# A decoder step on one core: the output projection as three products of split operands, its weights loaded and split in eight pieces

## The chip, the core and the metric

The kernel runs on one core of a Trainium2 chip, as one program with one launch. The metric is the device time of that program in microseconds, the median over the runs shown. PE is the matrix engine (TensorE), PEld its loads of the stationary operand, DVE the vector engine, ACT the scalar engine, POOL GpSimd, and SP the queue engine that issues most transfers.

## What is computed

One decoder layer over 1,024 prompt tokens and 8 sample tokens, in float32, width 1,024. Cut to the part around the change:

```python
h = rmsnorm(x, norm1_g)
sq, sk, sv, dq, dk, dv, ga, gb = project_inputs(h, pos, w_in, qn_g, kn_g)
o_sb  = sb_attn(sq, sk, sv, sb_bias)          # stick-breaking attention
o_dil = dil_attn(dq, dk, dv)                  # dilated windows
y_a = o_sb  @ w_br_a
y_b = o_dil @ w_br_b
x = x + (ga * y_a + gb * y_b) @ w_out         # <- the output projection, [1032 x 1024] @ [1024 x 1024]
x = x + moe(rmsnorm(x, norm2_g), ...)         # router, top 8 of 64 experts, shared expert
```

The change touches only how the product with `w_out` is computed, and how `w_out` comes into SBUF.

## The kernel before, in words

The program is a row of stages, each a block of its own with a barrier of all engines at its end: `phase_project` (input projection), `phase_windows` and `phase_stick` (attention), `phase_gate` (gates and the two branch products), `phase_out` (output projection, second norm, router logits), `phase_route` (top-k and the table of blocks), `phase_experts`, `phase_finish`. A stage can't begin, its transfers included, before the one ahead of it has ended.

**Float32 products in two ways.** Where a matmul takes float32 operands, the trace has two records for each matmul instruction. Where the operands are of the type `F32R` (fp32r in the rows), it has one. Three stages use `F32R` already, in the same pattern: ACT writes a rounded copy `hi` of an operand, DVE writes `lo = raw - hi`, and PE adds three products, hi x hi, hi x lo and lo x hi, into one PSUM tile. These are the input projection (lines 562 to 564, weights in `wring`, 128 x 512 outputs), the gates (lines 1460 to 1462) and the down product of the experts (line 2199).

**`phase_out` (from line 1550).** There are NT = 9 tiles of tokens, eight of 128 rows and a last one of 8. `mixT` holds the gated mix, already turned, as KC = 8 chunks of 128 contraction rows. It lies in the large buffer `turned`, as `h2T` does. The work of a tile `t`:

- PE, line 1630: for both halves `k` of the 1,024 output columns and all 8 chunks `c`, one float32 matmul with the stationary operand `mixT[:, c, tile]` and the moving operand `wo[:, c, 512 columns]`, into `pY[t % 2]`: 16 matmuls, thus 32 records. Then it signals `y_ready`.
- DVE, line 1687: `x1 = pY + x`, with the rows of `x` loaded again from DRAM (line 1603). ACT, line 1658: sum of squares of `x1`; line 1660: square root. DVE, line 1689: reciprocal; line 1693: `h2`.
- SP, lines 1608 and 1609: `x1` and `h2` to DRAM.
- PE, line 1640: eight transposes of `h2` into `pT`; ACT, line 1665: copy to `h2T`. PE, line 1647: router logits of the tile, 8 float32 matmuls of 64 columns.

PE's program runs as: products of tile `t`, transposes of tile `t - 1`, logits of tile `t - 2`. Before the products of `t >= 2` it waits for `x1` of tile `t - 2`, which frees the half of `pY`.

**How the stage begins.** SP issues one transfer for the whole of `w_out` (4 MB, line 1591), one for the gain of the norm (0.5 MB once broadcast, line 1592), one for the router weights (0.25 MB, line 1593), then two stores of zero rows (0.64 MB each, lines 1595 and 1596), then the `x` rows of tiles 0 and 1. The first three share one semaphore, and PE waits for all of it (`pe.wait_ge(w_in, 48)`) before its first matmul. ACT and DVE have nothing to do until tile 0 is through PE. POOL writes three small constants.

Of the kernel before, what the change touches and what calls it, by code (L numbers as in the profile page):

```python
# [49 lines left out]
def rows_of(t):  # L50
    return P if t < NT - 1 else NS
# [19 lines left out]
def build(nc, a, o):  # L71
# [22 lines left out]
    with ExitStack() as ctx:  # L94
        sb = lambda name, shape, dt=F32: ctx.enter_context(nc.sbuf_tensor(name, shape, dt))
        held = []

        def semaphore(name):
            held.append(nc.alloc_semaphore(name=name))
            return held[-1]  # L100

        scratch["semaphore"] = semaphore
        ident = sb("ident", [P, P])
        scores = sb("scores", [P, NT, E])
        expert_row = sb("expert_row", [1, NBLK + 1], I32)
        slot_info = sb("slot_info", [P, NBLK, 4], I32)
        with ExitStack() as attention:
            turned = attention.enter_context(nc.sbuf_tensor("turned", [P, 20, S], F32))
            phase_project(nc, a, o, scratch, ident, turned)
            odT = attention.enter_context(nc.sbuf_tensor("odT", [P, GW // P, T], F32))  # L110
            phase_windows(nc, a, o, scratch, ident, turned, odT)
            oT = attention.enter_context(nc.sbuf_tensor("oT", [P, SBH // 2, T], F32))
            phase_stick(nc, a, o, scratch, ident, turned, oT)

            nc.clear_and_free_semaphores(held)
            nc.all_engine_barrier()
            phase_gate(nc, a, o, scratch, turned, oT, odT)
            phase_out(nc, a, o, scratch, ident, turned, scores)
            phase_route(nc, a, o, scratch, ident, turned, scores, expert_row, slot_info)
        phase_experts(nc, a, o, scratch, ident, expert_row, slot_info)  # L120
        phase_finish(nc, a, o, scratch)
# [1428 lines left out]
def phase_out(nc, a, o, sc, ident, turned, scores):  # L1550

    flat = turned[:, :, :].rearrange("p a b -> p (a b)")
    h2T = flat[:, :KC * T].rearrange("p (c t) -> p c t", c=KC)
    mixT = flat[:, KC * T:2 * KC * T].rearrange("p (c t) -> p c t", c=KC)
    with ExitStack() as ctx:
        sb = lambda name, shape, dt=F32: ctx.enter_context(nc.sbuf_tensor(name, shape, dt))
        sem = sc["semaphore"]
        wo = sb("w_o", [P, KC, D])
# [5 lines left out]
        junk = sb("junk2", [P, D])  # L1564
        zero = sb("zero_row", [BLK // 5, D])
# [7 lines left out]
        w_in = sem("o_w_in")  # L1573
# [14 lines left out]
        with nc.Block() as block:  # L1588
            @block.sync
            def _(sp):  # L1590
                sp.dma_start(wo[:, :, :], a["w_out"][0].rearrange("(c p) n -> p c n", p=P)).then_inc(w_in, 16)
                sp.dma_start(gain[:, :], a["norm2_g"].broadcast_to([P, D])).then_inc(w_in, 16)
                sp.dma_start(wr[:, :, :], a["w_router"][0].rearrange("(p c) n -> p c n", c=KC)).then_inc(w_in, 16)
                sp.wait_ge(set_up, 3)
                sp.dma_start(sc["h2"][T:, :].rearrange("(p n) d -> p n d", n=5), zero[:, :].unsqueeze(1).broadcast_to([BLK // 5, 5, D])).then_inc(zero_out, 16)
                sp.dma_start(sc["x2"][T:, :].rearrange("(p n) d -> p n d", n=5), zero[:, :].unsqueeze(1).broadcast_to([BLK // 5, 5, D])).then_inc(zero_out, 16)
# [17 lines left out]
            @block.gpsimd  # L1614
            def _(pool):
                pool.memset(eps[:, :], EPS).then_inc(set_up, 1)
                pool.memset(zero[:, :], 0.0).then_inc(set_up, 1)
                pool.memset(scores[:, :, :], 0.5).then_inc(set_up, 1)

            @block.tensor  # L1620
            def _(pe):
                pe.wait_ge(w_in, 48)
                for t in range(NT + 2):
                    if t < NT:
                        m = rows_of(t)
                        if t >= 2:
                            pe.wait_ge(x1_ready, t - 1)
                        for k in range(2):
                            for c in range(KC):
                                last = pe.matmul(pY[:m, t % 2, k * 512:(k + 1) * 512], mixT[:, c, t * P:t * P + m], wo[:, c, k * 512:(k + 1) * 512],  # L1630
                                                 start=(c == 0), stop=(c == KC - 1))
                        last.then_inc(y_ready, 1)
# [10 lines left out]
                    if u >= 0:  # L1643
                        m = rows_of(u)
                        pe.wait_ge(h2T_ready, u + 1)
                        for c in range(KC):
                            last = pe.matmul(pR[:m, u // 8, (u % 8) * E:(u % 8 + 1) * E], h2T[:, c, u * P:u * P + m], wr[:, c, :],
                                             start=(c == 0), stop=(c == KC - 1))
# [3 lines left out]
            def _(act):  # L1652
                act.wait_ge(set_up, 3)
                for t in range(NT + 1):
                    if t < NT:
                        m = rows_of(t)
                        act.wait_ge(x1_ready, t + 1)
                        act.activation(junk[:m, :], x1[:m, t % 2, :], ACT.Square, accum_out=ss[:m, t:t + 1]).then_inc(ss_ready, 1)
                        act.wait_ge(ss_ready, t + 1)
                        act.activation(rms[:m, t:t + 1], ss[:m, t:t + 1], ACT.Sqrt, scale=1.0 / D, bias=eps[:m, :]).then_inc(rms_ready, 1)  # L1660
                    if t >= 1:
# [9 lines left out]
            def _(dve):  # L1671
# [8 lines left out]
                dve.wait_ge(w_in, 48)  # L1680
                for t in range(NT):
# [8 lines left out]
                    if t >= 2:  # L1690
# [3 lines left out]
                                             by_chunk(gain[:m, :]), ALU.mult, ALU.mult).then_inc(h2_ready, 1)  # L1694

# [683 lines left out]
```

## Time and profile before

| | before |
|---|---|
| median of 3 runs | 2507.28 us (2506.61 to 2510.26) |
| the profiled execution, its own time | 2507.1 us |
| span of its trace | 2505.3 us |
| PE busy | 2216.6 us, 88% of the span |
| DVE, ACT, POOL busy | 1013.7, 684.4, 802.8 us |
| granted TensorE clock, mean | 0.933 |
| `phase_out` in the trace | from 1210.9 to 1381.4 us |
| products of line 1630 | 256 records of 128 x 512 and 32 of the last tile |

Times in the rows are in microseconds from the start of the span unless marked ns. "Busy" is the time in which an engine had at least one instruction under way; matmuls overlap, so the spacing of their starts is their pace, and the duration of one is longer than that. The granted clock is given as a share of 2.4 GHz: 1.00 is 2.4 GHz and 0.50 is 1.2 GHz.

### The profile page before, as it was taken

To read this page: it belongs to the slowest core of one execution; us is meant where nothing else is said; L and a number is where in the kernel's file an instruction comes from. 1 tells how busy PE (TensorE), PEld (TensorE's weight loads), DVE (VectorE), ACT (ScalarE), POOL (GpSimd) and SP (SyncE) were. 2 spreads that over 40 slices of the span, in tenths; PEclk is the share of its full clock that TensorE was granted. 3 is DMA by queue.
4 is the path that set the end of the run, shared out by engine and by line. 5 is a ranking of instruction groups with operands and counts; after the bars stand their busy time and mean duration, and the time that the engine had idled before them with its cause. 6 is when DMAs were issued, how large, how long until landed. Compare 5 with 4: busy or idle time off the path is not lost. (4 is left out here: it accounts for less than half of the span.)

```text
span 2505.3 us, 35857 instructions
## 1 busy us (share of the span) xinstructions
PE 2216.6 (88%) x13110; PEld 1737.1 (69%) x13110; DVE 1013.7 (40%) x1695; ACT 684.4 (27%) x1156; POOL 802.8 (32%) x784
## 2 busy tenths in 40 slices
PE   7998499888599979999799771999999999999994
PEld 6776477677344438898454531898989888898983
DVE  4576778766354442111022441333333333333331
ACT  6221122145254542111011000233333333323231
POOL 2000033102555530111000074454545454555542
PEclk9999799958799989999899895999999999999997
DMA  6576611063345528881331143899999999999996
GB/s 209 190 233 213 219 34 35 29 200 121 126 135 160 159 83 288 281 281 42 135 108 61 57 136 133 273 326 318 327 324 321 324 321 322 320 328 316 326 314 175
DMA packets 182418, 520.08 MB, mean 208 GB/s; under 512 B 22942, under 2 KB 81752, under 8 KB 155880
## 3 DMA queue, kind: packets, MB, share of 16 engines
q1 hardware_dynamic: 137040, 369.24, 43.2%
q0 software_dynamic: 34912, 89.87, 14.3%
q10 hardware_dynamic: 10368, 59.73, 7.1%
q8 instruction: 55, 0.90, 0.2%
q14 instruction: 43, 0.35, 0.1%
HBM read 442.32 MB, written 124.65 MB: 226 GB/s over the span
## 5 line engine op out<-in xcount | busy, mean ns | idle before, releaser
L2182 PE MATMUL pG_e<-xT,w_e 128*128 128x160 f32 x4224 | 627.5, 302 | 2.4 <-issue 1.3
L2182 PEld LDWEIGHTS pG_e<-xT,w_e 128*128 128x128 f32 x4224 | 586.8, 197 | 29.4 <-issue 25.9
L2282 DVE TENSOR_TENSOR w_e_lo<-w_e,w_e_hi 128x2048 fp32r<-128x2048 f32 x66 | 151.4, 2294 | 342.0 <-ACT w_e_hi L2229 342.0
L562 PE MATMUL pP<-wring,hT_hi 128*128 128x512 f32 (+2 forms) x576 | 229.2, 398 | 45.9 <-DVE wring L498 43.5
L563 PE MATMUL pP<-wring,hT_hi 128*128 128x512 f32 (+2 forms) x576 | 223.9, 389 | 0.0
L564 PE MATMUL pP<-wring,hT_lo 128*128 128x512 f32 (+2 forms) x576 | 223.8, 389 | 0.0
L2131 POOL DMA_INDIRECT x_scratch<-y_e,target x66 | 106.7, 1617 | 341.6 <-ACT y_tail L2249 341.6
L2229 ACT ACTIVATE w_e_hi<-w_e 128x2048 fp32r<-128x2048 f32 x66 | 126.1, 1911 | 329.1 <-DMA w_e<-in_w_e_down 329.1
L2272 DVE COPY xT<-pX 128x512 f32<-128x512 f32 x132 | 90.7, 687 | 226.7 <-PE pX L2166 226.7
L355 POOL TENSOR_TENSOR sqr<-stage 128x512 f32<-128x512 f32 (+1 forms) x27 | 29.0, 1074 | 411.9 <-ACT stage L427 411.9
L562 PEld LDWEIGHTS pP<-wring,hT_hi 128*128 128x128 f32 (+1 forms) x576 | 105.9, 184 | 74.8 <-issue 45.0
L1460 PE MATMUL pG<-hg_hi,wg_hi 128*128 128x344 f32 x384 | 130.2, 339 | 16.1 <-DVE hg_lo L1521 16.1
L1630 PE MATMUL pY<-w_o,turned 128*128 128x512 f32 (+1 forms) x288 | 127.2, 601 | 17.9 <-DMA w_r<-in_w_router 17.9
L427 ACT ACTIVATE stage<-pP 128x512 f32<-128x512 f32 (+3 forms) x72 | 41.1, 570 | 338.3 <-PE pP L564 323.0
L2116 POOL DMA_INDIRECT rows<-h_scratch,index x66 | 109.6, 1660 | 54.4 <-POOL index L2113 51.0
L564 PEld LDWEIGHTS pP<-wring,hT_lo 128*128 128x128 f32 (+1 forms) x576 | 105.4, 183 | 29.2
L563 PEld LDWEIGHTS pP<-wring,hT_hi 128*128 128x128 f32 (+1 forms) x576 | 106.1, 184 | 26.7
L1461 PE MATMUL pG<-hg_lo,wg_hi 128*128 128x344 f32 x384 | 124.0, 323 | 0.0
L1462 PE MATMUL pG<-hg_hi,wg_lo 128*128 128x344 f32 x384 | 124.0, 323 | 0.0
L2248 ACT ACTIVATE y_e<-pY_e,target 128x1024 f32<-128x1024 f32 x66 | 73.6, 1115 | 179.8 <-DMA x_scratch<-y_tail,target 175.0
L1630 PEld LDWEIGHTS pY<-w_o,turned 128*128 128x128 f32 (+1 forms) x288 | 51.7, 182 | 87.6 <-issue 69.2
L1547 POOL TENSOR_TENSOR turned<-halves 128x344 f32<-128x344 f32 x24 | 27.8, 1160 | 263.1 <-DVE halves L1540 263.1
(271 smaller groups left out, 3788.9 us busy)
## 6 DMA issues: line engine op xcount, KB each, us to landing
w_e<-in_w_e_gate SPq DMA_DIRECT2D x66, 1024.0 KB, 8.3
w_e<-in_w_e_up SPq DMA_DIRECT2D x66, 1024.0 KB, 13.0
w_e<-in_w_e_down SPq DMA_DIRECT2D x66, 1024.0 KB, 6.8
turned<-in_cache_sb_kv SPq DMA_DIRECT2D x128, 256.0 KB, 3.4
vbuf<-in_cache_sb_kv SPq DMA_DIRECT2D x128, 256.0 KB, 3.0
out<-in_cache_win_kv ACTq DMA_DIRECT2D x8, 4094.0 KB
turned<-in_w_in ACTq DMA_DIRECT2D x56, 256.0 KB, 5.5
turned<-in_w_in SPq DMA_DIRECT2D x16, 512.0 KB, 8.8
```

The costliest lines, as they stand in the source:

```text
L562: pe.matmul(pP[:m, i % 4, :w], hi, w_hi(u), start=(c == 0), stop=False)
L563: pe.matmul(pP[:m, i % 4, :w], hi, w_lo(u), start=False, stop=False)
L564: last = pe.matmul(pP[:m, i % 4, :w], lo, w_hi(u), start=False, stop=(c == KC - 1))
L1460: pe.matmul(pG[:, i % 2, k, :NC], w_hi[:, r, c, :], hT_hi[:, c, cols], start=(c == 0), stop=False)
L1461: pe.matmul(pG[:, i % 2, k, :NC], w_hi[:, r, c, :], hT_lo[:, c, cols], start=False, stop=False)
L1462: last = pe.matmul(pG[:, i % 2, k, :NC], w_lo[:, r, c, :], hT_hi[:, c, cols], start=False, stop=(c == KC - 1))
L1630: last = pe.matmul(pY[:m, t % 2, k * 512:(k + 1) * 512], mixT[:, c, t * P:t * P + m], wo[:, c, k * 512:(k + 1) * 512], start=(c == 0), sto ...
L2116: pool.indirect_dma_start(rows[:, r, :], None, sc["h2"], bass.IndirectOffsetOnAxis(ap=index[:, r, 0:1], axis=0)).then_inc(rows_in[r], 16)
L2131: pool.indirect_dma_start(sc["x2"], bass.IndirectOffsetOnAxis(ap=target[:, r, 0:1], axis=0), y[:, :], None, compute_op=ALU.add).then_inc(y ...
L2182: last = pe.matmul(pG[:, k, f * BLK:(f + 1) * BLK], wv[:, c, f, :], xT[:, r, c, :], start=(c == 0), stop=(c == KC - 1))
L2229: act.activation(whi[:, r, :], w[:, r, 2, :], ACT.Copy).then_inc(whi_ready, 1)
L2282: dve.tensor_tensor(wlo[:, r, :], w[:, r, 2, :], whi[:, r, :].bitcast(F32), ALU.subtract).then_inc(wlo_ready, 1)
```

## The change

The product with `w_out` becomes three products of `F32R` operands. ACT writes `wo_hi` and DVE `wo_lo` from the raw weights, chunk by chunk, and for each tile ACT writes `mix_hi` and DVE `mix_lo` from `mixT`, one or two tiles ahead. PE issues 48 matmuls a tile in place of 16. `w_out` is loaded by eight transfers with a semaphore each; in tile 0 PE waits for each chunk's `lo`. PE no longer waits for the gain and the router weights ahead of its first product: DVE waits for the gain ahead of its first `x1`, PE for the router weights ahead of the first logits. The raw weights lie in `turned` now, over the place that `h2T` takes later. To make room, the two attention outputs `odT` and `oT` are freed ahead of `phase_out`, the sum of squares writes its unused result into `h2`, and the zero rows are a part of `h2`; so ACT waits for the stores of the zero rows before it writes `h2` of tile 1.

```diff
@@ build
+            branches.close()
             phase_out(nc, a, o, scratch, ident, turned, scores)
@@ phase_out
+    wo = flat[:, :KC * D].rearrange("p (c n) -> p c n", c=KC)
-        wo = sb("w_o", [P, KC, D])
+        wo_hi = sb("w_o_hi", [P, KC, D], F32R)
+        wo_lo = sb("w_o_lo", [P, KC, D], F32R)
+        mix_hi = sb("mix_hi", [P, 2, KC, P], F32R)
+        mix_lo = sb("mix_lo", [P, 2, KC, P], F32R)
-        junk = sb("junk2", [P, D])
-        zero = sb("zero_row", [BLK // 5, D])
+        zero = h2[:BLK // 5, 1, :]
@@ sync
-                sp.dma_start(wo[:, :, :], a["w_out"][0].rearrange("(c p) n -> p c n", p=P)).then_inc(w_in, 16)
-                sp.dma_start(gain[:, :], a["norm2_g"].broadcast_to([P, D])).then_inc(w_in, 16)
-                sp.dma_start(wr[:, :, :], a["w_router"][0].rearrange("(p c) n -> p c n", c=KC)).then_inc(w_in, 16)
+                for c in range(KC):
+                    sp.dma_start(wo[:, c, :], a["w_out"][0, c * P:(c + 1) * P, :]).then_inc(w_in[c], 16)
+                sp.dma_start(gain[:, :], a["norm2_g"].broadcast_to([P, D])).then_inc(gain_in, 16)
+                sp.dma_start(wr[:, :, :], a["w_router"][0].rearrange("(p c) n -> p c n", c=KC)).then_inc(wr_in, 16)
@@ tensor
-                pe.wait_ge(w_in, 48)
                 for t in range(NT + 2):
                     if t < NT:
                         m = rows_of(t)
+                        pe.wait_ge(mlo_ready, t + 1)
                         if t >= 2:
                             pe.wait_ge(x1_ready, t - 1)
-                        for k in range(2):
-                            for c in range(KC):
-                                last = pe.matmul(pY[:m, t % 2, k * 512:(k + 1) * 512], mixT[:, c, t * P:t * P + m], wo[:, c, k * 512:(k + 1) * 512],
-                                                 start=(c == 0), stop=(c == KC - 1))
+                        for c in range(KC):
+                            if t == 0:
+                                pe.wait_ge(wlo_ready, c + 1)
+                            terms = ((mix_hi, wo_hi), (mix_hi, wo_lo), (mix_lo, wo_hi))
+                            for n, (mt, wt) in enumerate(terms):
+                                for k in range(2):
+                                    last = pe.matmul(pY[:m, t % 2, k * 512:(k + 1) * 512], mt[:, t % 2, c, :m], wt[:, c, k * 512:(k + 1) * 512],
+                                                     start=(c == 0 and n == 0), stop=(c == KC - 1 and n == 2))
                         last.then_inc(y_ready, 1)
...
                         pe.wait_ge(h2T_ready, u + 1)
+                        if u == 0:
+                            pe.wait_ge(wr_in, 16)
@@ scalar
+                def high_mix(t):
+                    m = rows_of(t)
+                    if t >= 2:
+                        act.wait_ge(y_ready, t - 1)
+                    act.activation(mix_hi[:, t % 2, :, :m], mixT[:, :, t * P:t * P + m], ACT.Copy).then_inc(mhi_ready, 1)
+
+                high_mix(0)
+                for c in range(KC):
+                    act.wait_ge(w_in[c], 16)
+                    act.activation(wo_hi[:, c, :], wo[:, c, :], ACT.Copy).then_inc(whi_ready, 1)
+                high_mix(1)
...
-                        act.activation(junk[:m, :], x1[:m, t % 2, :], ACT.Square, accum_out=ss[:m, t:t + 1]).then_inc(ss_ready, 1)
+                        if t == 1:
+                            act.wait_ge(zero_out, 32)
+                        act.activation(h2[:m, t % 2, :], x1[:m, t % 2, :], ACT.Square, accum_out=ss[:m, t:t + 1]).then_inc(ss_ready, 1)
...
+                    if t + 2 < NT:
+                        high_mix(t + 2)
@@ vector
-                dve.wait_ge(w_in, 48)
+                def low_mix(t):
+                    m = rows_of(t)
+                    dve.wait_ge(mhi_ready, t + 1)
+                    if t >= 2:
+                        dve.wait_ge(y_ready, t - 1)
+                    dve.tensor_tensor(mix_lo[:, t % 2, :, :m], mixT[:, :, t * P:t * P + m], mix_hi[:, t % 2, :, :m].bitcast(F32),
+                                      ALU.subtract).then_inc(mlo_ready, 1)
+
+                low_mix(0)
+                for c in range(KC):
+                    dve.wait_ge(whi_ready, c + 1)
+                    dve.tensor_tensor(wo_lo[:, c, :], wo[:, c, :], wo_hi[:, c, :].bitcast(F32), ALU.subtract).then_inc(wlo_ready, 1)
+                low_mix(1)
+                dve.wait_ge(gain_in, 16)
...
+                    if t + 2 < NT:
+                        low_mix(t + 2)
```

## Rows read from the trace of the kernel before

**Rows 1.** The page: span and number of instructions.
```profile
span 2505.3 us, 35857 instructions
```

**Rows 2.** Groups by line and shape, 1208 to 1382 us: busy us, mean ns, idle ahead.
```profile
L1630 PE MATMUL pY<-w_o,turned 128*128 128x512 f32 x256 | 113.3, 602 | 17.9 <-DMA w_r<-in_w_router 17.9
L1647 PE MATMUL pR<-w_r,turned 128*128 128x64 f32 x128 | 17.0, 291 | 0.0
L1693 DVE SCALAR_TENSOR_TENSOR h<-x,rstd,gain 128x1024 f32<-128x1024 f32 x8 | 16.1, 2006 | 0.3
L1630 PE MATMUL pY<-w_o,turned 128*8 128x512 f32 x32 | 13.9, 592 | 0.0
```

**Rows 3.** Timeline of the stage: start, duration, instruction, idle time ahead of it.
```profile
1210.88 0.37 SPq L1591 DMA_DIRECT2D w_o<-in_w_out  x1
1226.47 29.61 PE L1630 MATMUL pY<-w_o,turned 128*128 128x512 f32 x64 [17.86 <-DMA w_r<-in_w_router]
1242.45 1.22 DVE L1687 TENSOR_TENSOR x<-pY,x_again 128x1024 f32<-128x1024 f32 x1 [32.86 <-PE pY L1630]
1248.77 0.33 SPq L1608 DMA_DIRECT2D x_scratch<-x  x1
1270.73 1.23 DVE L1687 TENSOR_TENSOR x<-pY,x_again 128x1024 f32<-128x1024 f32 x1 [9.63 <-PE pY L1630]
1287.13 1.23 DVE L1687 TENSOR_TENSOR x<-pY,x_again 128x1024 f32<-128x1024 f32 x1 [11.43 <-PE pY L1630]
```

**Rows 4.** Timeline of line 1630's loads: clock 0.50 first, then 1.00.
```profile
1229.20 0.34 PEld L1630 LDWEIGHTS pY<-w_o,turned 128*128 128x128 f32 x1 [0.52 <-issue]
1230.05 0.31 PEld L1630 LDWEIGHTS pY<-w_o,turned 128*128 128x128 f32 x1 [0.52 <-issue]
...
1238.33 0.19 PEld L1630 LDWEIGHTS pY<-w_o,turned 128*128 128x128 f32 x1 [0.24 <-issue]
...
1255.07 0.19 PEld L1630 LDWEIGHTS pY<-w_o,turned 128*128 128x128 f32 x1 [0.24 <-issue]
```

**Rows 5.** Timeline of PE in the input projection, clock 1.00, first and twentieth product.
```profile
99.78 0.40 PE L563 MATMUL pP<-wring,hT_hi 128*128 128x512 f32 x1
...
104.18 0.39 PE L564 MATMUL pP<-wring,hT_lo 128*128 128x512 f32 x1
```

**Rows 6.** Timeline of loads where the input projection begins, from second to twelfth product.
```profile
17.52 0.33 PEld L563 LDWEIGHTS pP<-wring,hT_hi 128*128 128x128 f32 x1
...
21.79 0.28 PEld L564 LDWEIGHTS pP<-wring,hT_lo 128*128 128x128 f32 x1
```

**Rows 7.** Groups by line of ACT and DVE, 935 to 1208 us: the gates' splits.
```profile
L1478 ACT ACTIVATE wg_hi<-turned 128x1024 fp32r<-128x1024 f32 x15 | 15.8, 1057 | 75.6 <-PE pG L1462 71.9 <-issue 3.3 <-DMA turned<-in_w_in 0.4
...
L1516 DVE TENSOR_TENSOR wg_lo<-turned,wg_hi 128x1024 fp32r<-128x1024 f32 x15 | 18.3, 1222 | 54.3 <-ACT wg_hi L1478 54.3
```

**Rows 8.** Stretches from 1210 us: length, the five engines' busy us, PEclk, DMA share, GB/s.
```profile
1210.00:1214.10 4.10, 0.00 (x0) 0.00 (x0) 0.00 (x0) 0.00 (x0) 2.07 (x4) 0.89 0.46 140
1210.00:1223.00 13.00, 0.00 (x0) 0.00 (x0) 0.00 (x0) 0.00 (x0) 2.07 (x4) 0.62 0.84 326
1210.00:1225.20 15.20, 0.00 (x0) 0.00 (x0) 0.00 (x0) 0.00 (x0) 2.07 (x4) 0.61 0.86 327
1210.00:1230.60 20.60, 4.13 (x5) 1.82 (x6) 0.00 (x0) 0.00 (x0) 2.07 (x4) 0.59 0.90 333
```

**Rows 9.** Transfers issued from 1208 to 1260 us: KB each, median us to landing.
```profile
h_scratch<-zero_row SPq DMA_DIRECT2D x1, 640.0 KB, 15.7
```

**Rows 10.** Issue to landing of ten stores into `x_scratch`: nine of x1, one of zeros.
```profile
DMA to landing us min/median/max: 2.6/2.7/16.6
```

**Rows 11.** Stretches of other stages, columns as in Rows 8.
```profile
1600.00:2020.00 420.00, 420.00 (x3105) 377.71 (x3104) 142.88 (x181) 128.40 (x153) 211.25 (x182) 1.00 1.00 322
```

**Rows 12.** Stretch of the input projection, products of line 562 alone.
```profile
250.00:300.00 50.00, 21.00 (x72) 13.40 (x72) 0.78 0.77 243
```

**Rows 13.** Who PE waited for, 1500 us to the end: total, times, longest.
```profile
PE pX L2166 <- DMA rows_tail<-h_scratch,index: 11.5, 1, 11.5
```

More of the change, by code:

```diff
@@ L109, in build @@
             phase_project(nc, a, o, scratch, ident, turned)
-            odT = attention.enter_context(nc.sbuf_tensor("odT", [P, GW // P, T], F32))
+            branches = ctx.enter_context(ExitStack())
+            odT = branches.enter_context(nc.sbuf_tensor("odT", [P, GW // P, T], F32))
             phase_windows(nc, a, o, scratch, ident, turned, odT)
-            oT = attention.enter_context(nc.sbuf_tensor("oT", [P, SBH // 2, T], F32))
+            oT = branches.enter_context(nc.sbuf_tensor("oT", [P, SBH // 2, T], F32))
             phase_stick(nc, a, o, scratch, ident, turned, oT)
@@ L1572, in phase_out @@
         pR = ctx.enter_context(nc.psum_tensor("pR", [P, 2, 512], F32))
-        w_in = sem("o_w_in")
+        w_in = [sem(f"o_w_in{c}") for c in range(KC)]
+        gain_in = sem("o_gain_in")
+        wr_in = sem("o_wr_in")
+        whi_ready = sem("o_whi_ready")
+        wlo_ready = sem("o_wlo_ready")
+        mhi_ready = sem("o_mhi_ready")
+        mlo_ready = sem("o_mlo_ready")
         x_in = [sem(f"o_x_in{i}") for i in range(2)]
@@ L1590, in _ @@
             def _(sp):
-                sp.dma_start(wo[:, :, :], a["w_out"][0].rearrange("(c p) n -> p c n", p=P)).then_inc(w_in, 16)
-                sp.dma_start(gain[:, :], a["norm2_g"].broadcast_to([P, D])).then_inc(w_in, 16)
-                sp.dma_start(wr[:, :, :], a["w_router"][0].rearrange("(p c) n -> p c n", c=KC)).then_inc(w_in, 16)
+                for c in range(KC):
+                    sp.dma_start(wo[:, c, :], a["w_out"][0, c * P:(c + 1) * P, :]).then_inc(w_in[c], 16)
+                sp.dma_start(gain[:, :], a["norm2_g"].broadcast_to([P, D])).then_inc(gain_in, 16)
+                sp.dma_start(wr[:, :, :], a["w_router"][0].rearrange("(p c) n -> p c n", c=KC)).then_inc(wr_in, 16)
                 sp.wait_ge(set_up, 3)
-                sp.dma_start(sc["h2"][T:, :].rearrange("(p n) d -> p n d", n=5), zero[:, :].unsqueeze(1).broadcast_to([BLK // 5, 5, D])).then_inc(zero_out, 16)
-                sp.dma_start(sc["x2"][T:, :].rearrange("(p n) d -> p n d", n=5), zero[:, :].unsqueeze(1).broadcast_to([BLK // 5, 5, D])).then_inc(zero_out, 16)
+                sp.dma_start(sc["h2"][T:, :].rearrange("(p n) d -> p n d", n=5), zero.unsqueeze(1).broadcast_to([BLK // 5, 5, D])).then_inc(zero_out, 16)
+                sp.dma_start(sc["x2"][T:, :].rearrange("(p n) d -> p n d", n=5), zero.unsqueeze(1).broadcast_to([BLK // 5, 5, D])).then_inc(zero_out, 16)
                 for t in range(NT + 1):
@@ L1616, in _ @@
                 pool.memset(eps[:, :], EPS).then_inc(set_up, 1)
-                pool.memset(zero[:, :], 0.0).then_inc(set_up, 1)
+                pool.memset(zero, 0.0).then_inc(set_up, 1)
                 pool.memset(scores[:, :, :], 0.5).then_inc(set_up, 1)
```

## The prediction

> **What bounds the kernel now.** I read the profile in this order: the page for the span [rows 1], the groups by line within `phase_out` for the size of the product [rows 2], then the timeline of the stage for what ends each wait [rows 3, 4].
>
> The stage has two parts. In the first, PE stands idle: the load of `w_out` is issued at 1210.88, and PE's first product starts at 1226.47, after an idle stretch that the transfer of `w_r` ended [rows 3]. `w_r` is the last of three transfers behind one semaphore. In the second, PE is the bound without a gap: the 32 records of a tile follow each other, and DVE's sum of tile 0 starts at 1242.45, of tile 2 at 1270.73, of tile 3 at 1287.13 [rows 3]. So the period is 16.40 us. DVE sat idle 11.43 us of it until PE was done [rows 3]. Whatever shortens PE's tile shortens the stage, until another chain fills the period.
>
> **Pace before.** At clock 1.00 the loads of line 1630 that start at 1238.33 and at 1255.07 have 39 gaps between them, 0.429 us each [rows 4]. Two records make one float32 matmul of 512 columns, 0.858 us, and a tile has 16: 13.73 us. At clock 0.50 the loads are 0.85 us apart (1229.20, 1230.05) [rows 4].
>
> **Pace after.** The same product already runs in the input projection: `F32R`, 128 x 512, hi and lo interleaved. From the first product at 99.78 to the twentieth at 104.18 are 19 gaps, 4.40 us, thus 0.2316 us for each product at clock 1.00 [rows 5]. At clock 0.50, ten gaps from 17.52 to 21.79 give 0.427 us [rows 6]. A tile after the change has 48 such products: 48 x 0.2316 = 11.12 us. The saving is 13.73 - 11.12 = 2.61 us a tile. It holds for the last tile of 8 rows too, as its 32 records took 13.9 us [rows 2]: the 512 moving columns set the time, not the rows.
>
> The Trainium skill ("TensorE: Matmul & The Clock Gate", section "Back-to-back issue gap") gives 512 / 2.4 + 2.5 = 216 ns for one pass at the full clock. By it a tile would take 10.4 us, and the kernel would end some 6 us earlier than I forecast. The row has 231.6 ns for this very pattern, so the row decides.
>
> **Tile 0, term by term.** First the bytes. 0.574 MB had moved by 1214.1 (4.10 us at 140 GB/s), 4.24 MB by 1223.0, 4.97 MB by 1225.2 [rows 8]. The weights are 4.19 MB, and with gain and `w_r` it is 4.98 MB. PE started 1.27 us after 1225.2, which I take for the time from the last byte to the signal. Served in order, piece 0 (0.524 MB) is in at 1214.0 and signalled at 1215.3; piece 7 is in at 1222.9 and signalled at 1224.2; the pieces come 1.27 us apart. That transfers are served in order shows in the store of zero rows, issued behind the weights: 15.7 us to landing for 640 KB [rows 9], where the typical store of 512 KB into the `x1` scratch took 2.7 [rows 10]. SP issues each of the eight in about 0.4 us (0.37 for the one there is) [rows 3], 3 us for all, well ahead of the data.
>
> Each piece then passes ACT and DVE. The gates' splits have the same 128 x 1024 shape: 1.06 us and 1.22 us [rows 7]. Both are below 1.27, so neither engine holds up the row of pieces. The splits of `mixT` for tile 0 (1.06 + 1.22) lie in the time before piece 0 lands. PE starts at 1215.3 + 1.06 + 1.22 + 0.1 = 1217.7. The granted clock fell while PE was idle (mean 0.62 from 1210 to 1223) [rows 8], and PE's first products before the change ran at 0.50 [rows 4]; the same holds here. The slow stretch lasted from 1226.47 to a little after 1230.05 there [rows 3, 4], and 4.7 us where the input projection began [rows 6]; I take 4.2. At 0.427 us that is 9.8 products; the other 38.2 take 8.85 us. PE ends tile 0 at 1217.7 + 4.2 + 8.85 = 1230.8. The data do not hold it up: piece 7 is split at 1224.2 + 2.3 = 1226.5, and its six products need 1.4 us more, thus 1227.9. Before, DVE's sum came at 1242.45, so PE's end was at about 1242.2. Gain on tile 0: 11.4 us.
>
> **What the change adds beside that.**
> - Per tile, ACT's copy of the mix (1.06) and DVE's difference (1.22) [rows 7]. The chain from the sum of tile 0 to the store of its `h2` took 1248.77 - 1242.45 = 6.3 us, with one table load in it [rows 3]. With DVE's 1.22 behind it, `mix_lo` of tile t + 2 is ready 7.6 us after PE has finished tile t. PE asks for it only after tile t + 1, at least 11.1 us later. Cost nothing. The cover is 3.5 us or more: what exceeds it would be paid once a tile.
> - ACT copies `h2T` 1.06 us later, for logits a whole tile away. Nothing.
> - `x` of tile 0 is now wanted 11.4 us earlier. It is behind the same bytes as before: 6.8 MB, and 6.86 had moved by 1230.6 [rows 8], so it is signalled at 1231.9. DVE's first sum is about 1 us late. `h2` of tile 0 is then ready at 1238.2, and PE asks for it at 1230.8 + 11.1 = 1241.9. Hidden, with 3.7 us to spare.
> - ACT waits for the zero rows before it writes `h2` of tile 1. The second of the two is issued at once behind the first (landing at 1228.1 by [rows 9] and the issue at 1212.40), and tile 1 comes at 1242. Nothing. The waits for gain and `w_r` end by 1226.5, ahead of their use.
> - The end of the stage is as it was: no split is left for it. The freeing of `odT` and `oT` moves addresses only.
>
> **What follows the stage.** From 1381 us on, everything is set in motion by the stage's end, and its transfers start with its own block. The loop of the experts is bound by PE (420.00 of 420.00 us busy) with the DMA share at 1.00 [rows 11]; neither sees the change. The gain is carried to the end whole.
>
> **Sum.** 11.4 + 8 x 2.61 = 32.3 us. The profiled execution took 2507.1 us (span 2505.3 [rows 1] and 1.8 around it), 0.2 below the median of the three runs. 2507.1 - 32.3 + 0.2 = 2475.0 us.
>
> **Bounds of the unknowns.** The slow stretch from none to 4.7 us: -1.9 to +0.2 us. The pace of the products: the down product of the experts has the least alike order, some 0.234 us; that is +1 us. Start of PE: 1 us either way. Run to run, those before differ by 3.6 us. So the likeliest case has 2471 to 2479 as its own range.
>
> **Rivals.**
> 1. *Each piece pays for itself.* If eight pieces don't overlap as one transfer does, each costs the 2.7 us of a lone store of this size [rows 10]: the last lands at 1210.9 + 21.6 = 1232.5, and tile 0 ends at 1232.5 + 2.3 + 1.4 = 1236.2, 5.4 us later. Time 2480.4. Against it speaks that DMA ran at share 0.86 up to 1225.2, the quiet start included, over three transfers in a row [rows 8]. Chance 0.09. The Trainium skill ("DMA: Bandwidth & Descriptors", section "Measured (HBM→SBUF, 128 partitions, SWDGE, issued from GpSimd)") says to batch transfers to at least 1 MiB for 75% of peak, which speaks against pieces of 512 KB. It is this rival; [rows 8] don't bear it out for transfers that are queued one behind another.
> 2. *The pieces don't come in order*, so that splitting the load does nothing: the first usable one is signalled with the last, by 1226.4 as `w_r` was [rows 3]. PE starts at 1228.8 and ends tile 0 at 1241.8; the gain there is 0.4 us in place of 11.4. Time 2486. Against it: the late zero rows [rows 9]. Chance 0.07.
> 3. *Slower: the clock is lost.* PE waits piece by piece in tile 0, and later on the splits. The input projection, with the same pattern and waits on splits, had a stretch of 50 us at a granted clock of 0.78 [rows 12]. A product at clock 0.50 costs 0.427 - 0.232 = 0.195 us more. With the clock at 0.50 throughout, the 422 products other than those already counted slow cost 82 us: 2557 us. It turns the sign once 32.3 / 0.195 = 166 of them, three and a half tiles, run slow. Against it: at half clock the six products of a piece take 2.6 us and pieces come each 1.27 us, so PE doesn't wait in tile 0 once started, and later the cover is 3.5 us a tile. Chance 0.03.
> 4. *Given back later.* The experts begin with a wait of 11.5 us for gathered rows [rows 13], and their loop has no DMA to spare [rows 11]. One more such wait: 2486.5. Nothing in the change feeds it. Chance 0.04.
> 5. *Faster than forecast*: a slow stretch near nothing and an earlier first piece, 2470. Chance 0.05.
>
> **Chances and range.** The forecast keeps 0.72. 2470 to 2486 holds it, rival 1 and about half of rivals 2, 4 and 5, some 0.88; its lower end is the fast case and its upper end rival 2, and neither can be drawn in without losing a case. A measurement of this kernel can tell about 0.2%, 5 us, from no change. Faster by more: all cases but rival 3, and of it the part with under 3 tiles slow, less what none of them names: 0.96. Within: 0.01. Slower: 0.03.
>
> **What would show it.** In the profile after: eight loads of `w_out` and PE's first product at about 1217.7, 6.8 us after the first load's issue; the loads of line 1630's successor 0.427 us apart for some ten products and 0.232 from then on; DVE's first sum near 1232; a period of 13.8 us in place of 16.4; no idle PE ahead of `mix_lo`. Wrong would be: a first product after 1224 (rival 2), gaps between the pieces' products at full clock in tile 0 that leave its end after 1233 (rival 1), PEclk under 1.00 in the tiles from 1 on (rival 3), or a stage 32 us shorter with a total that isn't (rival 4).

## The result, and the profile after

| | before | after |
|---|---|---|
| median | 2507.84 us (4 runs, 2506.61 to 2510.26) | 2471.79 us (4 runs, 2470.16 to 2475.73) |
| profiled execution, span | 2507.1, 2505.3 us | 2471.59, 2469.7 us |
| first load of `w_out` to the first transfer of the next stage | 1210.88 to 1381.51: 170.63 us | 1209.36 to 1344.17: 134.81 us |

The ratio is 0.9853, 95% interval 0.9839 to 0.9868: 36 us less. The forecast was 2475.0 in 2470 to 2486.

Of the spans' difference of 35.6 us, 35.8 lie in the stage itself. What is ahead of it was 1.5 us shorter, what follows was 1.7 us longer, and neither is touched by the change. In the kernels below, the stage's own length repeats within about 2 us, while its first load starts anywhere from 1207.7 to 1215.4. So I read the stage, from its first load (times with a plus sign), and the total only with its interval. Each length of a stage below is that of one trace.

The page after, to be read with [rows 1]: there are 346 more instructions, and the granted clock is as it was.

```profile
span 2469.7 us, 36203 instructions
PE 2189.0 (89%) x13254; PEld 1760.6 (71%) x13254; DVE 1033.4 (42%) x1712; ACT 700.6 (28%) x1173; POOL 804.2 (33%) x784
```

Groups by line and shape, 1208 to 1350 us, to be read with [rows 2] and [rows 7]. 256 records of one line have become three times 128; the splits cost what the gates' did; and PE's idle time ahead of the products is 8.5 us in place of 17.9.

```profile
L1646 PE MATMUL pY<-w_o_hi,mix_hi 128*128 128x512 f32 x128 | 40.8, 400 | 8.5 <-DVE w_o_lo L1724 8.5
L1646 PE MATMUL pY<-w_o_lo,mix_hi 128*128 128x512 f32 x128 | 40.0, 394 | 0.0
L1646 PE MATMUL pY<-w_o_hi,mix_lo 128*128 128x512 f32 x128 | 39.9, 393 | 0.0
...
L1724 DVE TENSOR_TENSOR w_o_lo<-turned,w_o_hi 128x1024 fp32r<-128x1024 f32 x8 | 9.8, 1225 | 3.4 <-ACT w_o_hi L1680 3.1
L1733 DVE TENSOR_TENSOR x<-pY,x_again 128x1024 f32<-128x1024 f32 x8 | 9.8, 1225 | 49.7 <-PE pY L1646 44.0 <-DMA x_again<-in_x_prompt 5.5
...
L1680 ACT ACTIVATE w_o_hi<-turned 128x1024 fp32r<-128x1024 f32 x8 | 8.5, 1060 | 4.7 <-DMA turned<-in_w_out 4.7
```

Timeline of the stage after, to be read with [rows 3]:

```profile
1209.36 3.81 SPq L1603 DMA_DIRECT2D turned<-in_w_out  x8
1213.12 1.06 ACT L1680 ACTIVATE w_o_hi<-turned 128x1024 fp32r<-128x1024 f32 x1 [2.67 <-DMA turned<-in_w_out]
1215.58 1.19 PE L1646 MATMUL pY<-w_o_hi,mix_hi 128*128 128x512 f32 x2 [8.47 <-DVE w_o_lo L1724]
...
1222.54 1.06 ACT L1680 ACTIVATE w_o_hi<-turned 128x1024 fp32r<-128x1024 f32 x1 [0.22 <-DMA turned<-in_w_out]
...
1231.54 1.23 DVE L1733 TENSOR_TENSOR x<-pY,x_again 128x1024 f32<-128x1024 f32 x1 [5.54 <-DMA x_again<-in_x_prompt]
1237.98 0.33 SPq L1620 DMA_DIRECT2D x_scratch<-x  x1
1238.92 1.03 PE L1656 MATMUL pT<-ident,h 128*128 128x128 f32 x8
...
1305.27 1.23 DVE L1733 TENSOR_TENSOR x<-pY,x_again 128x1024 f32<-128x1024 f32 x1 [7.46 <-PE pY L1646]
1318.86 1.23 DVE L1733 TENSOR_TENSOR x<-pY,x_again 128x1024 f32<-128x1024 f32 x1 [8.49 <-PE pY L1646]
1332.36 1.21 DVE L1733 TENSOR_TENSOR x<-pY,x_again 8x1024 f32<-8x1024 f32 x1 [8.46 <-PE pY L1646]
...
1344.17 0.36 SPq L1847 DMA_DIRECT2D before_r<-in_before  x1
```

The first piece is at ACT at +3.8 and the eighth at +13.2. ACT takes them in the order of issue, and its wait for each of the eight was ended by a transfer, 1.24 to 1.81 us after the one before, so they also came in that order. PE starts at +6.2; before it was +15.6. The period of a tile is 13.59 us in place of 16.40, and DVE still idles 7.5 us of it until PE is done (8.5 in the last two rows: no split of a later tile is left there). PE is the bound as before. And DVE's first sum waited 5.5 us for the `x` rows. `h2` of tile 0 was on its way out at 1237.98, and PE asked for it at 1238.92: 0.9 us of cover.

Timeline of PE's loads at the stage's start. Each row is two loads; 0.76 for two is clock 0.50, 0.42 is clock 1.00. The slow stretch is seven products long.

```profile
1217.85 0.76 PEld L1646 LDWEIGHTS pY<-w_o_hi,mix_hi 128*128 128x128 f32 x2
1218.70 0.42 PEld L1646 LDWEIGHTS pY<-w_o_lo,mix_hi 128*128 128x128 f32 x2
```

### The profile page after: what moved, and what is told of

Same layout as the page of the kernel before. It is cut to its first block and busy times, and to the rows that moved or that the text cites. A ratio compares the mean times of both kernels' runs of the same rounds, so it can differ in the third digit from the quotient of the medians.

```text
span 2469.7 us, 36203 instructions
## 1 busy us (share of the span) xinstructions
PE 2189.0 (89%) x13254; PEld 1760.6 (71%) x13254; DVE 1033.4 (42%) x1712; ACT 700.6 (28%) x1173; POOL 804.2 (33%) x784
## 5 line engine op out<-in xcount | busy, mean ns | idle before, releaser
L2181 POOL DMA_INDIRECT x_scratch<-y_tail,target x66 | 104.6, 1585 | 20.1 <-issue 20.1
L750 DVE TENSOR_SCALAR low<-pZ,bias 128x512 f32<-128x512 f32 (+3 forms) x96 | 54.9, 613 | 123.2 <-PE pZ L906 123.1
```

## The experiments

The edits stand against the changed kernel, except in the second. Their totals are told beside a run of the kernel before on the same chip.

### One half at a time

One transfer, the three products:

```diff
-                for c in range(KC):
-                    sp.dma_start(wo[:, c, :], a["w_out"][0, c * P:(c + 1) * P, :]).then_inc(w_in[c], 16)
+                sp.dma_start(wo[:, :, :], a["w_out"][0].rearrange("(c p) n -> p c n", p=P)).then_inc(w_in[0], 16)
...
-                    act.wait_ge(w_in[c], 16)
+                    act.wait_ge(w_in[0], 16)
```

> The changed kernel with its weights loaded by one transfer and one semaphore; the three products stay. The changed kernel took 2471.8 us. My theory (two separate gains: an early start worth about 10 us in tile 0, and a shorter PE tile worth 2.8 us in each): PE starts 15.7 us after the stage's first load in place of 6.2, tile 0 ends near 28.3 us after it in place of 18.7, the tiles after it keep their period of 13.6 us, and the time is about 2481. Rival (transfer order: the pieces are no earlier than the whole, PE's early start comes from dropping gain and router weights from the wait): time within 2 us of 2471.8. Rival (the pieces cost transfer time): a little faster than 2471.8.

Eight pieces, the product in float32 (against the kernel before; the loads and the later waits for the gain and the router weights are those of the change):

```diff
-                pe.wait_ge(w_in, 48)
...
-                        for k in range(2):
-                            for c in range(KC):
+                        for c in range(KC):
+                            if t == 0:
+                                pe.wait_ge(w_in[c], 16)
+                            for k in range(2):
```

> The kernel before with only the second half of the change: eight pieces with a semaphore each, chunks outermost on PE, gain and router weights waited for later; the product stays in float32, and there are no splits. My theory: PE starts about 3.8 us after the first load, tile 0 ends at about 19.6 in place of 31.4 us, the tiles after it keep 16.4 us, and the time is 2507.8 - 11.8 = 2496. Together with the run of one load it shows whether the two halves add up: 11.8 + (2507.8 - 2481) = 38.6 would be over the 36 of the whole, since the longer tile 0 hides a little of the load. Rival (the early start is worth something only with the shorter products): 2505 or more.

| | PE's first product | DVE's first sum | stage | total |
|---|---|---|---|---|
| before | +15.6 | +31.6 | 170.6 | |
| three products alone | +15.5 | +28.7 | 144.1 | 2477.9, ratio 0.9869 (0.9852 to 0.9885) |
| eight pieces alone | +3.7 | +21.2 | 159.3 | 2496.0, ratio 0.9942 (0.9925 to 0.9958) |
| the change | +6.2 | +22.2 | 134.8 | 0.9853 (0.9839 to 0.9868) |

Against the kernel before, the products alone shorten the stage by 26.6 us and the pieces alone by 11.3, where the whole has 35.8. The expectation put such a difference down to the length of tile 0. The rows show another reason: both kernels also drop the wait for the gain and the router weights, so it is counted twice. With one transfer, all of `w_out` was there at +13.0 (first row below), where PE had waited until +15.6 before. The dropped wait is thus worth 2.6 us, and in the kernels with three products the two splits of the first chunk take 2.5 back (+13.0 to +15.5). What the pieces give by themselves is 15.5 - 6.2 = 9.3 us, and 144.1 - 134.8 is the same 9.3.

In the first kernel ACT gets its first piece only with the last byte; the idle stretch of PE is back:

```profile
1223.66 5.79 ACT L1679 ACTIVATE w_o_hi<-turned 128x1024 fp32r<-128x1024 f32 x6 [11.93 <-DMA turned<-in_w_out]
...
1226.12 1.19 PE L1645 MATMUL pY<-w_o_hi,mix_hi 128*128 128x512 f32 x2 [17.73 <-DVE w_o_lo L1723]
```

The rival that the early start comes from the dropped wait for gain and router weights falls: this kernel doesn't wait for them either, and starts at +15.5. The total was 2477.9 us where I had expected 2481, and the total alone would not have shown the loss, which is 9.3 us against the first run of the change and 7.4 against its second. The changed kernel run again on another chip had 0.9872 (0.9853 to 0.989), within the interval of this one. The stage showed it.

### PE as the bound: 16, 48 and 64 products

```diff
-                            terms = ((mix_hi, wo_hi), (mix_hi, wo_lo), (mix_lo, wo_hi))
+                            terms = ((mix_hi, wo_hi), (mix_hi, wo_lo), (mix_lo, wo_hi), (mix_lo, wo_lo))
```

> The changed kernel with the fourth product too (lo x lo), 64 in place of 48 a tile. If PE is the bound in each tile: 16 x 0.2265 = 3.6 us more a tile, the period 17.2 us in place of 13.6, in nine tiles 32.6 us, and the time about 2504, near the time of the kernel before. Rival (another chain, the splits or the x rows, sets part of the period of 13.6 us): less than that by the part.

```diff
+                            terms = ((mix_hi, wo_hi),)
```

> The changed kernel with only the product hi x hi, 16 a tile: two of the three terms are left out, so the product with w_out is less exact; all splits are still made. PE's tile is 3.6 us of products and 3.0 of transposes and logits, thus 6.6 us. The rest of the stage then shows what comes next after PE. My theory: the split of tile t + 2 waits for the sum and norm of tile t (about 6.4 us behind it on DVE), and the x rows of tile t + 1 are issued about 7 us after tile t - 1 and take 5.8 us to land, so the period is 6.6 to 7.5 us, and the time is 2471.8 - 8 x 6.5 - (2 to 4) = about 2417. Rival (a chain just under 13.6 us has been hidden by PE): a period over 9 us.

| products a tile | period | stage | total, one run |
|---|---|---|---|
| 16 | 6.34 us | 85.2 | 2425.2 |
| 48 | 13.59 us | 134.8 | |
| 64 | 17.22 us | 168.0 | 2502.5 |

The period falls on one line: (17.22 - 13.59) / 16 = 0.227 us for each product, and (13.59 - 6.34) / 32 = 0.227. So nothing but PE sets the period, over all this range; with 64 products the stage was 33.2 us longer, where 32.6 was expected. Even at 6.34 us PE is without a gap in the steady tiles, where DVE's sum now follows its last one within 0.2 us:

```profile
1259.65 1.03 PE L1656 MATMUL pT<-ident,h 128*128 128x128 f32 x8
1259.85 1.23 DVE L1733 TENSOR_TENSOR x<-pY,x_again 128x1024 f32<-128x1024 f32 x1 [0.21 <-PE pY L1646]
1260.53 1.90 PE L1665 MATMUL pR<-w_r,turned 128*128 128x64 f32 x16
...
1262.23 3.92 PE L1646 MATMUL pY<-w_o_hi,mix_hi 128*128 128x512 f32 x16
```

I had expected 2417 for 16 products, a stage 55 us shorter than in the change; it was 49.6 shorter, and the rest of the eight us between lies outside the stage. What the stage lacks is at its beginning. There, tile 0 and tile 1 gained only 1.1 us together (the second sum at +28.6 in place of +29.8): the loads set tile 0's end, and then PE waited 6.2 us for `h2` of tile 0.

### The x rows late

```diff
+                for i in range(2):
+                    sp.dma_start(pad[:, i, :], a["x_prompt"][0, i * P:i * P + P]).then_inc(pad_in, 16)
```

> The changed kernel with 1 MB more loaded (into a buffer that nothing reads) ahead of the x rows of tile 0. In the change DVE waited for these rows until 1231.54, and the store of h2 of tile 0 was issued at 1237.98, 0.9 us before PE had ended tile 1 and asked for it: the cover was 0.9 us, where I had predicted 3.7. My theory: the rows come 2.7 us later, PE then waits about 1.8 us ahead of the transposes of tile 0, and the stage is longer by that. Rival (the cover is not used up, as PE has other work): no wait ahead of the transposes.

DVE's first sum came at +25.6 in place of +22.2, 3.4 us later. PE waited 2.1 us ahead of the transposes of tile 0. So far as expected. But the stage took 139.6 us, 4.8 more than in the change, not 2. The timeline of PE behind the wait shows the rest:

```profile
1239.64 1.10 PE L1661 MATMUL pT<-ident,h 128*128 128x128 f32 x8 [2.09 <-DVE h L1744]
1240.69 0.93 PE L1651 MATMUL pY<-w_o_hi,mix_hi 128*128 128x512 f32 x2
1241.43 1.05 PE L1651 MATMUL pY<-w_o_lo,mix_hi 128*128 128x512 f32 x2
1242.28 1.05 PE L1651 MATMUL pY<-w_o_hi,mix_lo 128*128 128x512 f32 x2
1243.13 1.05 PE L1651 MATMUL pY<-w_o_hi,mix_hi 128*128 128x512 f32 x2
1243.99 0.85 PE L1651 MATMUL pY<-w_o_lo,mix_hi 128*128 128x512 f32 x2
1244.67 0.63 PE L1651 MATMUL pY<-w_o_hi,mix_lo 128*128 128x512 f32 x2
```

The same in stretches (length, PE, PEld, DVE, ACT, POOL, PEclk, DMA share, GB/s):

```profile
1238.00:1240.00 2.00, 0.35 (x3) 0.36 (x4) 2.00 (x2) 0.33 (x1) 0.00 (x0) 1.00 0.00 0
1240.00:1242.00 2.00, 2.00 (x11) 1.57 (x10) 1.77 (x2) 0.20 (x1) 0.00 (x0) 0.76 0.80 322
1242.00:1244.00 2.00, 2.00 (x7) 1.52 (x6) 0.65 (x2) 1.97 (x4) 0.00 (x0) 0.50 0.98 279
1244.00:1246.00 2.00, 2.00 (x9) 1.64 (x8) 2.00 (x2) 1.14 (x2) 0.00 (x0) 0.88 0.46 186
```

Behind a wait of 2.1 us and small transposes the granted clock went from 1.00 to 0.50 and came back some 3 us later, and that cost about as much again as the wait: the transposes of tile 0 were 2.3 us later than in the change (+31.9 against +29.6), and DVE's sum of tile 2 was 4.25 us later (+45.8 against +41.5), so 1.9 us came from the slow products. The last half microsecond of the 4.8 is at the stage's end. The rival (PE has other work, no wait) fell.

That a wait of this length costs twice itself is not a rule, though. In the input projection, ahead of anything that these kernels change, PE waits once for DVE about 138 us into the span, 2.1 to 3.3 us in the 13 traces. Behind it the granted clock fell to 0.50 in nine of them, after the shortest of these waits too (2.09 us in the run with busy DVE and ACT), and stayed at 1.00 in four (3.00, 2.70, 2.65 and 2.30 us). The changed kernel is one of the four. Its wait, and the same stretch in it and in the kernel before, which waited 3.27 us:

```profile
138.15 0.47 PE L564 MATMUL pP<-wring,hT_hi 128*128 128x512 f32 x1 [3.00 <-DVE wring L500]
134.00:144.00 10.00, 7.00 (x34) 5.35 (x32) 8.53 (x11) 1.74 (x4) 0.00 (x0) 1.00 0.44 136
134.00:144.00 10.00, 6.72 (x26) 5.12 (x24) 8.88 (x11) 1.62 (x3) 0.00 (x0) 0.83 0.45 136
```

So the length of such a wait doesn't decide it in these traces, and what does stays open.

### The slow stretch at the beginning

Twelve extra matmuls ahead of tile 0, and `x` of tile 0 loaded ahead of the zero rows:

```diff
+                sp.dma_start(x[:, 0, :], a["x_prompt"][0, :P]).then_inc(x_in[0], 16)
                 sp.wait_ge(set_up, 3)
...
+                for _ in range(WARM):
+                    pe.matmul(pR[:, 1, :P], ident[:, :], ident[:, :], start=True, stop=True)
```

> The changed kernel again, unaltered, beside the next one on the same chip: 2472 us, and tile 0 with a slow stretch of PE's clock of 2.5 to 4.7 us.

> The changed kernel with two additions: PE runs 12 matmuls of a 128 x 128 identity in float32 while the first piece is on its way (their result is overwritten later), and the x rows of tile 0 are loaded ahead of the zero rows. If what the granted clock does at the stage's start follows from PE's idle time before it: the clock is at 1.00 from the first product or soon after, the seven slow products of the change (0.427 us each in place of 0.227) are gone, and the time is 1 to 1.5 us below the run beside it. DVE's wait for x of tile 0 (5.5 us, until 3.5 us after tile 0 had ended) is gone and brings nothing. Rival (the pieces set the end of tile 0 once PE is fast): the gain is under 0.5 us, with gaps between the products of tile 0. Both are near what five rounds can tell; the trace decides.

The same with 24:

> The run with 12 extra matmuls showed them to take 2.9 us, end 3.1 us before PE's first product, and leave the clock at 0.50 for the first products. This one has 24, which should end 0.1 to 0.4 us before that product. If the clock follows PE's idle time just ahead: it is at 1.00 in tile 0 from the first product, the slow stretch (2.7 to 5.8 us in the four kernels with the change so far) is gone, tile 0 ends 17.5 us after the first load in place of 18.7 to 20.6, where the pieces then hold it up, and the time is 1 to 2.5 us below the change. Rival (extra work of this kind does not count, or the pieces hold PE up): tile 0 ends at 18.7 or later.

| kernel | gaps at half pace in tile 0 | load of tile 1's first product | stage |
|---|---|---|---|
| the change, first run | 7 | +18.5 | 134.8 |
| four orders (below) | 10 | +18.8 | 134.5 |
| the change again | 14 | +19.7 | 136.7 |
| 12 extra matmuls, `x` early | 14 | +19.7 | 136.6 |
| busy DVE and ACT (below) | 14 | +19.8 | 136.7 |
| 24 extra matmuls, `x` early | none | +17.6 | 133.7 |

The change again had 2474.9 us, ratio 0.9872, and 12 extra matmuls 2475.7 beside it, ratio 0.9881 (0.9864 to 0.9897): no difference. The length of the slow stretch changes from run to run, from 7 to 14 products, and each slow product puts the end of tile 0 some 0.2 us later. It was 6.0 us long in the change run again, where I had expected 2.5 to 4.7. This is 1.4 of the 2 us in which the stage repeats. Most of the rest is in the last tile, where the clock falls a little earlier or later behind a wait of 2.4 us: the transposes and logits that end the stage take 5.9 us in the first run of the change (1337.31 to 1343.17) and 6.4 when it ran again. Twelve extra matmuls ran in 2.9 us and left PE idle for 3.1 us ahead of its first product, and the clock was at 0.50 again. The run tells when it fell: it was at 1.00 while the extra matmuls ran and for 1.8 us behind them, and at 0.50 when the first product came (columns as above).

```profile
1214.00:1216.00 2.00, 0.15 (x2) 0.00 (x0) 0.16 (x1) 1.06 (x1) 0.00 (x0) 1.00 0.98 401
1217.00:1219.00 2.00, 1.78 (x4) 1.49 (x5) 1.41 (x3) 1.13 (x2) 0.00 (x0) 0.50 1.03 420
```

DVE's wait for `x` was gone and nothing came of it, as expected. With 24, PE was idle for 0.36 us only, and the slow stretch is gone:

```profile
1212.68 5.60 PE L1637 MATMUL pR<-ident 128*128 128x128 f32 x48 [2.31 <-PEq L1419]
1218.64 0.70 PE L1650 MATMUL pY<-w_o_hi,mix_hi 128*128 128x512 f32 x2 [0.36 <-DVE w_o_lo L1728]
1219.17 0.63 PE L1650 MATMUL pY<-w_o_lo,mix_hi 128*128 128x512 f32 x2
...
1222.11 0.73 PE L1650 MATMUL pY<-w_o_hi,mix_hi 128*128 128x512 f32 x2 [0.47 <-DVE w_o_lo L1728]
```

Of the two things in which 24 differ from 12, more work and a shorter idle stretch, the second is the likelier cause, as 12 had the clock at 1.00 too for as long as they ran; no run varies one alone. As the last row shows, the pieces now hold PE up: that rival holds in part, and so a part of what the clock gives is lost to it. This is the shortest stage, 0.8 to 3 us under the others. Its total had a ratio of 0.9844 (0.9821 to 0.9868): the intervals of the changed kernel's two runs overlap it, so in the total it isn't shown to be faster. The chip of that run was slower by some 30 us in all kernels, 2538.9 before and 2501.9 for this one; that difference lies outside this stage.

### Four pieces

```diff
-                for c in range(KC):
-                    sp.dma_start(wo[:, c, :], a["w_out"][0, c * P:(c + 1) * P, :]).then_inc(w_in[c], 16)
+                for c in range(0, KC, 2):
+                    sp.dma_start(wo[:, c:c + 2, :], a["w_out"][0, c * P:(c + 2) * P, :].rearrange("(c p) n -> p c n", p=P)).then_inc(w_in[c], 16)
...
-                    act.wait_ge(w_in[c], 16)
+                    act.wait_ge(w_in[c - c % 2], 16)
```

> The changed kernel with w_out loaded in four pieces of 1 MB in place of eight of 0.5 MB; the splits are made chunk by chunk as before. My theory (pieces are served in order at the full rate, so their size changes only when the first two chunks are there): PE's first product 1.3 us later than in the change (7.5 us after the first load in place of 6.2), tile 0 no more than 1.5 us later, the time within 2 us of the change. Rival (each piece pays a cost of its own, so that fewer are better): the last chunk's split starts earlier after the first load than in the change, where it began 13.2 us after it, and the time falls by up to 2 us.

PE's first product was at +7.5, as expected. Here ACT begins the last two chunks at +12.7 and makes them one behind the other, thus the last at about +13.7, where eight pieces had it at +13.2:

```profile
1214.36 2.00 ACT L1680 ACTIVATE w_o_hi<-turned 128x1024 fp32r<-128x1024 f32 x2 [3.98 <-DMA turned<-in_w_out]
...
1222.04 2.01 ACT L1680 ACTIVATE w_o_hi<-turned 128x1024 fp32r<-128x1024 f32 x2 [0.56 <-DMA turned<-in_w_out]
```

The rival by which each piece pays for itself falls: the last split is no earlier. The last data were there at +12.7, and the eighth piece came between +12.4 and +13.9 in the nine traces with eight pieces and splits, so a price of a piece, if there is one, is too small to be seen. Tile 1's first product was loaded at +20.8, 2.3 us later than in the first run of the change, where I had allowed 1.5; 1.3 of it is the later start, and 1.0 is a slow stretch of 12 products in place of 7. The stage took 136.0 us, and the ratio was 0.9861 (0.9834 to 0.9889).

### The pace of the products

Four orders in one kernel: tiles 3 and 4 take the banks in turn with another stationary operand each time, tiles 5 and 6 one bank, as in the input projection, and tiles 7 and 8 one bank with another stationary operand each time.

```diff
+                        elif t in (3, 4):
+                            for c in range(0, KC, 2):
+                                for swap in range(2):
+                                    for n, (mt, wt) in enumerate((hi_hi, hi_lo, lo_hi)):
+                                        for k in range(2):
+                                            q = c + (k ^ swap)
...
+                        elif t in (5, 6):
+                            for k in range(2):
+                                for c in range(KC):
+                                    for n, (mt, wt) in enumerate((hi_hi, hi_lo, lo_hi)):
...
+                        else:
+                            for k in range(2):
+                                for n, (mt, wt) in enumerate((hi_hi, hi_lo, lo_hi)):
+                                    for c in range(KC):
```

> The products of the change took 0.2265 us each where I had 0.2316 from the input projection, 1.3 us a tile in all 9 tiles with the slow stretch aside. This kernel gives the same products in four orders. Tiles 0 to 2: as in the change (the two PSUM banks in turn, the stationary operand kept for 4, then 2 products). Tiles 3 and 4: banks in turn, another stationary operand at each product. Tiles 5 and 6: one bank for 24 products, stationary operand kept for 2, as in the input projection. Tiles 7 and 8: one bank, another stationary operand at each product. If the bank sets the pace: 0.2265, 0.2265, 0.2316, 0.2316. If the stationary operand sets it, by how often it changes (1 in 3, 1 in 1, 2 in 3, 1 in 1): 0.2265, 0.2365, 0.2316, 0.2365. If neither does (operands' places in SBUF): 0.2265 in all. Time within 3 us of 2472 in any case, no verdict from it.

The period was 13.59 us in every full tile from 3 to 7, whatever the order. So neither bank nor stationary operand sets the pace. Within a tile, though, the gap is 0.230 to 0.235 us for about the first 2.5 us and 0.2267 after it, also in the order of the input projection, whose products keep 0.2316 throughout [rows 5]. That this is the traffic of ACT and DVE, which work in just that part of the tile, was tried:

```diff
+                        if t == 6:
+                            for i in range(3):
+                                act.activation(pad[:, i, :], gain[:, :], ACT.Copy)
...
+                    if t == 3:
+                        for i in range(3):
+                            dve.tensor_tensor(flat[:, 2 * KC * T + i * D:2 * KC * T + (i + 1) * D], gain[:, :], gain[:, :], ALU.add)
```

> Within a tile of the changed kernel the gap between products is 0.230 to 0.232 us for the first three us and 0.2267 after it; the order of banks and stationary operands doesn't change that. The first part is when ACT and DVE do the norm and the splits. Here DVE adds the gain to itself into a spare place three times after its work on tile 3 (3.7 us more), and ACT copies the gain three times after its work on tile 6 (3.2 us more). If DVE's or ACT's traffic in SBUF slows PE: the slower gap goes on for as long in that tile, 0.07 us a tile at most, and the other tiles stay as they are. If it does not: the gaps are as in the change, and what sets the slower one stays open. Time as the change.

DVE's extra work ran from 1272.99 for 3.49 us, ACT's from 1311.42 for 2.94 us, and PE's gaps from 1272.6 and from 1312.5 on were 0.2267 all the same. It isn't the traffic in SBUF of either of them alone. That both engines read PSUM early in the tile wasn't tried. What makes the gap of 0.231 us stays open; it is worth 0.1 us a tile here.

## Why the prediction was right, point by point

- **PE bounds the tile before and after; its pace comes from another stage of the same kernel.** Right. The period fell by 2.81 us where I had 2.61. The mis-sized term is the gap of 0.2316 us from [rows 5]: here it was 0.2267 for most of a tile. 8 x 0.2 = 1.6 us of the 3.5 us that I had too little. Another 1.3 are in tile 0 and half a microsecond is at the stage's end, both below.
- **Pieces are served in order at the full rate.** Right: +3.8 for the first, +13.2 for the eighth, where I had +4.4 and +13.3. PE's start at +6.2 where I had +6.8.
- **Tile 0's end.** I had +19.9, it was +18.7 in the profiled run (the start of tile 1's first product at 1228.0), by the earlier start and by a slow stretch of 3 us in place of 4.2. With the slow stretch of other runs it was 1.3 us later, thus where I had it: the profiled run had a short one by luck. The earlier start in it, 9.4 us where I had 8.8, is 9.3 for the pieces and 2.6 for the dropped wait, less 2.5 for the first splits; I hadn't priced the dropped wait apart.
- **The cover for `x`.** Wrong in size: 0.9 us where I had 3.7. `x` of tile 0 came 1.2 us later than I had it (+22.2 against +21.0), which put `h2` at +28.6 against +27.3, and PE asked for it 1.5 us earlier (+29.6 against +31.0). That it cost nothing was luck and not the margin I had worked out. In the run with late rows, which used it up, the stage lost twice the wait. I had priced a stall at its own length, and it can cost more.
- **The splits are hidden.** Right: no wait for `mix_lo` in any tile, even at a period of 6.34 us.
- **Nothing at the end of the stage.** From the last sum to the next stage it was 11.8 us where it had been 12.4, and 12.4 when the change ran again. The half microsecond is the moment at which the granted clock falls in the last tile: the eight small transposes took 0.66 us there, 1.01 before and 1.02 in the change again, and the 32 records of logits 5.28, 5.48 and 5.48. It isn't the change's.
- **The gain is carried to the end.** Right: stage 35.8 us, total 36.
- **Rivals.** Each piece pays: no, by the four pieces. Out of order: no, by ACT's starts. Given back later: no, but what follows the stage differs by 4 us between runs by itself. The clock is lost: not in the change; the run with late rows shows that this was a real mechanism, which a wait of only 2 us can be followed by.

## What to carry to other kernels

A float32 product that bounds a stage costs 1.72 us for 1,024 columns here, and its three fp32r products 1.36: look for the pace in a stage of the same kernel that does it already, and check that both splits fit in the period. Where a stage begins with a load that PE waits for, cut the load along PE's order of use, which was worth 9.3 us here, and wait for nothing that the first product doesn't need, which was worth 2.6. And don't price a stall of PE at its length alone: in one run 2.1 us of waiting cost 4, and behind a wait of 2.1 to 3.3 us in the input projection the clock fell in nine traces of 13.

## What the runs showed of the hardware that I had not expected

- A wait of 2.1 us amid full work took the granted clock from 1.00 (2.4 GHz) to 0.50 (1.2 GHz), for about 3 us of products at 0.427 us each. An idle stretch of 3.1 us behind 2.9 us of extra matmuls did the same; one of 0.36 us did not. At one and the same wait in the input projection the clock fell in nine traces (waits of 2.09 to 3.27 us) and stayed in four (2.30 to 3.00 us).
- The slow stretch behind nearly the same idle time (8.5 and 8.4 us) lasted 7 and 14 products in two runs of the same kernel.
- The gap between fp32r products of 512 columns is 0.2267 or some 0.231 us at the same granted clock, in one tile, independent of the bank, of the stationary operand, and of SBUF traffic of ACT alone or DVE alone.
- A piece of 0.5 MB in a row of them has no cost that can be seen against one of 1 MB: eight come 1.35 us apart, four 2.56, and all of `w_out` was there at +13.2, +12.7 and, in one transfer, +13.0.
